# Conditioning vectors kept as rows and stored once; branch weights and first gates loaded one stage earlier

## What is computed

```
mod = silu(c) @ w_ada + b_ada                      # c: 9 rows of 1024, w_ada: 1024 x 6144
sh1, sc1, gt1, sh2, sc2, gt2 = split(mod, 6)       # six vectors of 1024 for each condition
h   = rmsnorm(x, g_norm_mix) * (1 + sc1) + sh1
out = (g_ssm * (y @ w_br_ssm) + g_attn * (attn @ w_br_attn)) @ w_out
x   = x + gt1 * out
h   = rmsnorm(x, g_norm_ffn) * (1 + sc2) + sh2
x   = x + gt2 * hier_moe(h)
```

## Time and profile before

| what | value |
|---|---|
| median of 3 runs | 1555.7 us (1551.64 to 1557.76) |
| the profiled execution | 1549.84 us |
| its span | 1548.1 us |
| PE busy in the span | 1399.3 us (90%) |
| DVE, ACT, POOL busy | 492.7, 287.2, 113.9 us |
| mean granted TensorE clock | 0.944 of full |

### The profile page before, as it was taken

The page is one execution under the profiler, slowest core; times in us unless marked ns, Lnnn a source line. Parts: engine busy times, 40 slices in busy tenths (PEclk is TensorE's granted clock), DMA queues, the critical chain, the costliest instruction groups (busy, mean ns, idle before and its releaser), DMA issues. The chain is left out here.

```text
span 1548.1 us, 20491 instructions
## 1 busy us (share of the span) xinstructions
PE 1399.3 (90%) x8575; PEld 923.4 (60%) x8575; DVE 492.7 (32%) x1069; ACT 287.2 (19%) x667; POOL 113.9 (7%) x116
## 2 busy tenths in 40 slices
PE   4999999999999899998999989999986999999930
PEld 3556667899888666665567666688872333333310
DVE  4300001113433125670092234443653421111108
ACT  4100000002333221112321222111221111111103
POOL 0000000000011014001000000000001001000033
PEclk9999999998999699998999999999986999999965
DMA  9333222322442333233320039231036899999848
GB/s 314 127 122 123 82 82 93 100 72 90 156 176 79 96 115 121 76 123 78 55 83 15 9 137 301 85 134 41 28 143 258 297 378 416 416 415 414 327 125 238
DMA packets 131421, 253.18 MB, mean 164 GB/s; under 512 B 22505, under 2 KB 96889, under 8 KB 123122
## 3 DMA queue, kind: packets, MB, share of 16 engines
q1 hardware_dynamic: 106082, 189.67, 34.7%
q0 software_dynamic: 10560, 33.50, 6.6%
q10 hardware_dynamic: 14688, 28.71, 5.0%
HBM read 204.96 MB, written 49.63 MB: 164 GB/s over the span
## 5 line engine op out<-in xcount | busy, mean ns | idle before, releaser
L352 PE MATMUL psum<-h_t,ring 128*128 128x352 f32 x576 | 174.7, 466 | 2.7 <-DVE h_t L503 2.7
L352 PEld LDWEIGHTS psum<-h_t,ring 128*128 128x128 f32 x576 | 110.4, 193 | 65.8 <-issue 6.9
L996 PE MATMUL psum<-h_t,ring 128*128 128x352 f32 x480 | 146.8, 464 | 3.0 <-PEq L624 3.0
L996 PEld LDWEIGHTS psum<-h_t,ring 128*128 128x128 f32 x480 | 90.8, 192 | 52.0 <-issue 4.2
L2076 PE MATMUL psum<-ring,big 128*128 128x256 f32 x512 | 114.1, 381 | 2.1 <-PEq L1734 2.1
L2076 PEld LDWEIGHTS psum<-ring,big 128*128 128x128 f32 x512 | 96.0, 190 | 15.5 <-issue 3.1
L2183 PE MATMUL psum<-w_gate_up,u_rows 128*32 128x512 f32 x608 | 101.7, 609 | 3.0 <-ACT u_rows L2304 1.1
L368 PE MATMUL psum<-ring,h_t 128*128 128x256 f32 (+1 forms) x432 | 103.1, 395 | 0.0
L2183 PE MATMUL psum<-ring,u_rows 128*32 128x512 f32 x576 | 101.7, 599 | 0.9 <-ACT u_rows L2304 0.9
L368 PEld LDWEIGHTS psum<-ring,h_t 128*128 128x128 f32 (+1 forms) x432 | 90.5, 266 | 8.7 <-issue 1.2
L2205 PE MATMUL psum<-big 128*32 128x512 f32 x736 | 83.7, 595 | 0.8 <-DVE big L2611 0.8
(11 more groups left out here) (460 smaller groups left out, 1815.9 us busy)
## 6 DMA issues: line engine op xcount, KB each, us to landing
big<-in_w_exp_down SPq DMA_DIRECT2D x32, 1024.0 KB, 10.7
ring<-in_w_ada SPq DMA_DIRECT2D x24, 1024.0 KB, 7.3
w_gate_up<-in_w_exp_gate SPq DMA_DIRECT2D x13, 1024.0 KB
w_gate_up<-in_w_exp_up SPq DMA_DIRECT2D x13, 1024.0 KB
ring<-in_w_exp_gate SPq DMA_DIRECT2D x13, 1024.0 KB, 6.7
ring<-in_w_exp_up SPq DMA_DIRECT2D x13, 1024.0 KB, 10.0
tmp_expert_rows<-zero_rows POOLq DMA_DIRECT2D x12, 1024.0 KB, 4.5
ring<-in_w_in SPq DMA_DIRECT2D x11, 1024.0 KB, 8.6
```

What stands on the lines that cost most here:

```text
L352: m = nc.tensor.matmul(bank[(e + j) % NB][:, 0:CW], w[:, k, c * P:(c + 1) * P], ht3[:, k, j * CW:(j + 1) * CW], start=(k == 0), stop=(k == ...
L996: m = T_.matmul(bank[4 + u % 4][:, 0:CW], w_[:, k, c0:c0 + P], ht3[:, k, j * CW:(j + 1) * CW], start=(k == 0), stop=(k == KT - 1))
```

## The change

- In stage 1 the ada blocks 8 to 23 are no longer copied whole. DVE copies the four partial results (9 partitions x 256) into `part`, counts `s_ac` behind the fourth, adds them, adds the result to the bias that POOL has loaded into `vec` (`ada_rows` again), and for the blocks of gain2 multiplies by (1 + .) * g_norm_ffn. `turn_ada(range(32), 24)` and the add into `mod_t` are gone. Behind its k stores POOL stores `vec` once as one row for the prompt, and four times for the samples (8 rows of 16 KB each), into two new scratch tensors, and waits for all five.
- In stage 4 SP loads the branch weights and the gates of the first three merge units into `h_t`, once the 18 late gate matmul groups are done.
- In stage 5 the spreading, the transposes and the copies are gone; merge units start at once. In place of the prompt's x rows, SP loads the vectors as rows (prompt rows broadcast to 128 partitions).
- In stage 6 SP first issues the 8 loads of the prompt's x rows, ahead of the router weights, the samples' x rows and the first expert. The first tile waits for its own row load and the vectors, the third tile for all of them.

```diff
@@ stage 1, POOL @@
+                    pool.wait_ge(s_adt, 5)
+                    pool.wait_ge(s_ssq, 2)
+                    pool.dma_start(vec, I["b_ada"][0:1, 2 * D:6 * D].to_broadcast([1 + DEC_B, 4 * D])).then_inc(s_vin, 16)
+                    pool.dma_start(g_vec, I["g_norm_ffn"][0:1, :].to_broadcast([1 + DEC_B, D])).then_inc(s_vin, 16)
                     out_k = {0: "k0", 1: "k1", 2: "k2"}
...
                         pool.wait_ge(s_ksl, 16 * (n + 1))
+                    pool.wait_ge(s_vready, 1)
+                    pool.dma_start(scratch["vector_p"], vec[0:1, :]).then_inc(s_vout, 16)
+                    for t in range(DEC_T):
+                        pool.dma_start(scratch["vector_s"].rearrange("(b t) c -> t b c", t=DEC_T)[t], vec[1:1 + DEC_B, :]).then_inc(s_vout, 16)
+                    pool.wait_ge(s_vout, 16 * (1 + DEC_T))
@@ stage 1, PE @@
-                    pe.wait_ge(s_kt_ev, len(k_jobs))
-                    turn_ada(range(32), 24)
@@ stage 1, DVE @@
                     def copy_ada(b):
                         dve.wait_ge(s_ada, b + 1)
+                        if b < 8:
+                            V.tensor_copy(ada_rows[:, b * WB:(b + 1) * WB], ada_bank(b)).then_inc(s_ac, 1)
+                            return
+                        for x in range(4):
+                            m = V.tensor_copy(part[:, x, :], ada_bank(b)[32 * x:32 * x + 1 + DEC_B, :])
+                        m.then_inc(s_ac, 1)
+                        dve.wait_ge(s_ac, b + 1)
                         if b == 8:
-                            dve.wait_ge(s_adt, 5)
-                        V.tensor_copy(ada_rows[:, (b if b < 8 else b - 8) * WB:(b + 1 if b < 8 else b - 7) * WB],
-                                      ada_bank(b)).then_inc(s_ac, 1)
+                            dve.wait_ge(s_vin, 32)
+                        cols = slice((b - 8) * WB, (b - 7) * WB)
+                        c.step(dve, V.tensor_tensor(part[:, 0:2, :], part[:, 0:2, :], part[:, 2:4, :], ALU.add))
+                        c.step(dve, V.tensor_tensor(part[:, 0, :], part[:, 0, :], part[:, 1, :], ALU.add))
+                        c.step(dve, V.tensor_tensor(vec[:, cols], vec[:, cols], part[:, 0, :], ALU.add))
...
-                    dve.wait_ge(s_adt, 6)
-                    V.tensor_tensor(mod_t[:, 16:48, :], bank[6][:, 0:288].rearrange("p (k c) -> p k c", c=9),
-                                    prm_t[:, 16:48].unsqueeze(2).to_broadcast([P, 32, 9]), ALU.add).then_inc(s_modv, 1)
@@ stage 4, SP @@
+                    sp.wait_ge(s_lgt, LATE)
+                    sp.dma_start(w_bs, I["w_br_ssm"][0].rearrange("(k p) c -> p k c", p=P)).then_inc(s_br, 16)
+                    sp.dma_start(w_ba, I["w_br_attn"][0].rearrange("(k p) c -> p k c", p=P)).then_inc(s_br, 16)
+                    for u in range(GL):
+                        load_gates(sp, u)
                     sp.wait_ge(s_fxe, 1)
@@ stage 5, SP @@
-                        if 7 <= u < 7 + TT:
-                            sp.dma_start(x2[:, u - 7, :], I["x_prompt"][0, (u - 7) * P:(u - 6) * P, :]).then_inc(s_xr5, 16)
+                        if 8 <= u < 16:
+                            v, x0 = VEC[(u - 8) // 2], VEC_COL[VEC[(u - 8) // 2]]
+                            if u % 2 == 0:
+                                sp.dma_start(row_p[v], scratch["vector_p"][:, x0:x0 + D].to_broadcast([P, D])).then_inc(s_vec[0], 16)
+                            else:
+                                sp.dma_start(row_s[v], scratch["vector_s"][:, x0:x0 + D]).then_inc(s_vec[1], 16)
@@ stage 5, PE @@
-                        for k in range(KT):
-                            T_.transpose(bank[b0 + k // 4][:, (k % 4) * P:(k % 4 + 1) * P], src[:, k, 0:1].to_broadcast([P, P]), ident[:, :])
-                            m = T_.transpose(bank[b0 + 2 + k // 4][0:NS, (k % 4) * P:(k % 4 + 1) * P], ex[:, v, k, :], ident[:, :])
@@ stage 6, SP and DVE @@
+                for t in range(TT):
+                    sp.dma_start(x2[:, t, :], I["x_prompt"][0, t * P:(t + 1) * P, :]).then_inc(s_xr5[min(t, 1)], 16)
...
-                        dve.wait_ge(s_xr5, 16 * TT)
+                        dve.wait_ge(s_vec[0], 64)
+                        dve.wait_ge(s_vec[1], 64)
+                        dve.wait_ge(s_xr5[0], 16)
+                    if i == 2:
+                        dve.wait_ge(s_xr5[1], 16 * (TT - 1))
```

More of the change, by code:

```diff
@@ L95, in build @@
         dec_mask = [sb(f"dec_mask{g}", [P, (128, 256, 64)[g] + NS]) for g in range(GROUPS)]
[L96 removed]
+        mod_t = sb("mod_t", [P, 2 * KT, 1 + DEC_B])
         prm_t = sb("prm_t", [P, 80])
@@ L1717, in x2_of @@
             return x2[:, t, :] if t < TT else x2_s
[L1719 removed]
         s_w5 = [sem(f"weights5_{i}_loaded") for i in range(RING)]
[L1721 to L1723 removed]
+        s_xr5 = [sem("first_x_rows_again"), sem("x_rows_again")]
+        s_vec = [sem("prompt_vectors_loaded"), sem("sample_vectors_loaded")]
         s_mu, s_md = sem("merge_unit_in_psum"), sem("merge_unit_done")
```

64 lines of the change are left out of this document (23 added, 41 removed).

## The result

| | before | after |
|---|---|---|
| median of 20 runs, us | 1553.88 (1551.28 to 1558.11) | 1559.34 (1555.38 to 1563.58) |
| profiled execution, us | 1549.84, span 1548.1, clock 0.944 | 1560.56, span 1558.8, clock 0.936 |

The ratio is 1.0029, with a 95% interval of 1.002 to 1.0038: the changed kernel is slower by some 4.5 us, less than the 0.5% that the prediction counted as a difference. The forecast was 5.5 us faster, 1550.2, which rested on a median of 1555.7 from 3 runs (20 runs give 1553.9); 1559.3 lies above its range. Executions of one kernel differ by some 7 to 12 us here.

What follows compares the result with a forecast made beforehand. PE was taken to set the end up to about 1180 us, with its waits and stage barriers. +10.3 + 0.5 - 4.2 + 0.6 - 12.7 = -5.5 us gave 1550.2 us, range 1540 to 1557.

Steps and rivals of the forecast that it cites:

- Ada pairs, the waits: Stage 1: four DVE copies for one start each pair's second block 1.29 us later, eight pairs, +10.3 us.
- Ada pairs, the clock: Stage 1 rival: longer pauses drop PE to 1.2 GHz, 1.7 us per pair, +13.6, 1563.8 us; chance 0.09.
- k turns behind the pairs: Stage 1, behind v0 and v1: k turn waits for DVE's copy behind the pair's chains, 0.3 us twice, +0.5.
- End of stage 1: Small matmuls gone, but POOL's sample stores, taken as 10 us, hold the barrier: gain 4.2 us (1.7 to 11.4).
- Clock at stage 2's start: Stage 2's start: PE comes from an 8 us idle stretch, 1.2 us more at half clock, +0.6 us.
- Start of stage 5: Merge begins without transposes, first matmul at 905.95 instead of 918.64, pause 3.05 us: gain 12.7 us.
- I take no drop: Start of stage 5: PE's clock stays at full behind the 3.05 us pause; a drop would cost up to 3.1 us.
- Stage 4 loads, stage 6 loads: Stages 4 to 6: moved weight, gate, vector and x row loads stay covered by other work, 0 us.

Runs made afterwards that it cites:

- e1_one_copy: Changed kernel with each ada block first copied whole out of PSUM, PE let go behind that, then the four copies from this buffer: 1544.62 us, ratio 0.9939.
- the two narrow probes: Changed kernel with the sample stores as eight stores of four rows, from partitions 4 to 7 or 2 to 5, output wrong: 1568.71 and 1560.28 us, one run each.
- e4_loads_in_merge: Changed kernel with branch weights and first gates loaded at the start of stage 5 again, not in stage 4: 1565.74 us, ratio 1.009.
- e8_filled_wait: Changed kernel with 12 extra matmuls into an unread bank ahead of the second block of each ada pair: 1551.42 us, ratio 0.9993.
- e5_before_four_copies: Kernel before with only the one copy of ada blocks 8 to 23 made four copies of 32 partitions: 1569.9 us, ratio 1.0108.
- e3_both: Changed kernel with one whole copy out of PSUM in the ada pairs and the five vector stores spread over k jobs 10 to 14: 1534.12 us, ratio 0.9869.
- e7_two_banks: Changed kernel with the five stores spread and a second PSUM bank for the second block of six ada pairs: 1523.52 us, ratio 0.9811.
- e9_filled_barrier: The kernel of e7_two_banks with two more matmuls into an unread bank at the end of stage 4: 1526.02 us, ratio 0.983 to the kernel before.
- p1_rows_4_7: Changed kernel with the four sample stores made eight stores of four rows, all from partitions 4 to 7, output wrong: 1568.71 us, one run.
- e6_one_sample_store: Changed kernel with the eight sample rows stored once and repeated four times by the load in stage 5: 1545.96 us, ratio 0.9945.

## Why the prediction was wrong

- **Ada pairs, the waits** (+10.3): right to the hundredth, 1.93 us six times, and 1.95 in the two pairs of the v blocks.
- **Ada pairs, the clock** (left out of the sum, a rival with a chance of 0.09): this is the step that failed. The prediction argued that a pause of 2.12 us ahead of stage 6 had left the clock at full, so that 1.93 us would. But that was one look at an event that goes either way: of thirteen traces, the pause ahead of stage 6 (2.12 to 2.16 us in all) is followed by slow matmuls in six. The rival's price for one pair, 1.7 us, was right (1.69); it hit three pairs of the changed kernel and not eight. Cost: 5.1 us, confirmed by the shorter, the filled and the added pause.
- **k turns behind the pairs** (+0.5): one stall of 0.16 us was seen. Right in kind; the longer chain of e1_one_copy showed the full one.
- **End of stage 1** (-4.2, measured -2.3): which engine holds the barrier was right, and so was the time of landing: 376.6 is 7.8 us behind PE's last v matmul, where the sum had 8.05 (355.5 against 347.45). That the time was right is in part luck: 10 us were a choice between 2.5 and 12.5, by a rate halved for 8 partitions, and the probes put it down to the 256 KB that leave partitions 4 to 7. The step that failed is the end of it: 0.4 us were allowed from the landing to stage 2, and it took 2.5. In the two narrow probes it took 2.8, with one sample store 2.2. No row shows what fills this time.
- **Clock at stage 2's start** (+0.6): PE's first two groups, up to 386.50, took 7.38 us against 6.18 (360.12 to 366.30), +1.2.
- **Start of stage 5** (-12.7): the pause is 2.94 us against a forecast of 3.05, a gain of 12.8. But "I take no drop" was wrong: in all nine traces with this pause the clock fell, and the first eight records took 4.1 to 4.3 us for 2.60. Cost: 1.7 us. It was the nearer of two neighbours again, taken from single events.
- **Stage 4 loads, stage 6 loads** (0): right. e4_loads_in_merge prices the cover at 10 us, and stage 6 waits for no row of x: its first DVE wait is one for PE.

Timeline of DVE at the first tile of stage 6 in the kernel after:

```profile
1029.26 1.23 DVE L2413 TENSOR_TENSOR big<-psum,u_rows 128x1024 f32<-128x1024 f32 x1 [13.60 <-PE psum L2083]
```

The parts close on the measured result. What the pairs cost by themselves (16.8), less the gap of stage 1 (2.3) and the start of stage 5 (12.8 - 1.7 = 11.1), with the clock at stage 2's start (1.2), makes +4.6 us; measured were +4.5. That it is so close is luck, since the 16.8 is known to some 4 us. By the traces alone, the waits and the stores would have left a gain of 4.6 us (+10.3 + 0.2 - 2.3 - 12.8), near the forecast of 5.5; the clock behind the pauses that the change made or moved took 8.0 us back, 5.1 in the pairs, 1.7 at stage 5 and 1.2 at stage 2, which leaves +3.4.

That stage 6 took 3.5 us longer in the trace of after is not put down to the change: e1_one_copy, e4_loads_in_merge and e8_filled_wait have the same code there and took 542.0 to 542.2 us, as before, and e5_before_four_copies, with the code of before there, took 545.0.

## What to carry to other kernels

- A wait on TensorE costs its own length and, at the 1.9 us and more of these runs, often a stretch at half clock behind it. Price both, and where the pause cannot go, fill it with matmuls into a bank that nobody reads: here eight times 1.5 us of useless work, in time that was idle anyway, saved 5.6 us.
- Let the producer go after the cheapest copy that frees the bank, or give it a second bank; split the data afterwards. With the stores spread as well, the same conditioning rows bring 20 to 29 us where the first version lost 4.5.
- How long a store of a few rows holds a barrier goes by the partitions that it leaves from. Store such rows once and repeat them in the load, or issue them units ahead of the barrier.

## What the runs showed of the hardware

**Pauses and the clock.** Behind pauses of 0.66 us or less, 30 of 30 q and k blocks behind ada pairs ran at full clock (before, e1_one_copy, e3_both, e7_two_banks, e8_filled_wait and e9_filled_barrier, five each). Behind 1.92 to 1.94 us, 20 of 35 were slow: three of five in six kernels, two in p1_rows_4_7, and which ones changed from trace to trace. Behind the same pauses, 1.93 to 1.95 us, with v blocks following, it was 3 of 25 (two in e6_one_sample_store, one in p1_rows_4_7); why fewer, no run shows. Behind 2.12 to 2.16 us at stage 6 it was 6 of 13; behind 2.94 us at stage 5, each time. Behind the 2.31 us of e6_one_sample_store at stage 2 the clock held. A fall in the pairs nearly always cost 1.69 us, half of some 3.4 us at 1.2 GHz.

**Not all falls need a pause.** Windows of PE in the kernel after, in stage 6, where before shows 1.00 in both places:

```profile
1113.45:1123.45 10.00, 9.25 (x45) 0.83 0.00 0
1133.45:1143.45 10.00, 10.00 (x58) 0.83 0.00 0
```

The first follows a pause of 0.75 us, the second none, only matmuls of few columns (36 to 46). The six traces whose stage 6 began slowly have both of these falls. So has e5_before_four_copies, whose stage 6 began at full clock; of the other six, four have the second alone and two, before and e7_two_banks, neither. What ties them was not tried. Between 36 and 42 us of stage 1, too, the clock fell in 11 of 13 traces, with no pause of PE over 0.83 us from 30 us on. So a short pause is no assurance outside the places counted above.

**Narrow stores.** Stores of four rows went out at 27 GB/s from partitions 4 to 7 and at 52 GB/s from partitions 2 to 5, at the same mean busy share of the DMA engines, 0.26.
